# Column sums of the norm inside the last slab, high and low halves of the next weights moved, and sixteen unread products on TensorE

## The reference

```python
for l in range(2):
    sh, sc, gt = adaln(cond, w_ada[l], b_ada[l])      # one set for context, one for latent tokens
    h = y * (1.0 + sc) + sh
    o = even_mixer(h, ...) if l == 0 else odd_mixer(h, ...)
    y = layernorm(ALPHA * y + gt * o, ln_g[l], ln_b[l])
```

## Time and profile before

| | us |
|---|---|
| median of 3 runs | 2573.54 |
| lowest, highest | 2573.10, 2576.51 |
| the profiled execution | 2572.51 |
| its span, first to last instruction | 2570.9 |
| TensorE busy | 2521.2 (98%) |
| VectorE, ScalarE, GpSimd busy | 1943.4, 929.9, 924.0 |
| mean granted TensorE clock | 0.99 |

### The profile page before, as it was taken

The page is one execution under the profiler, slowest core; times in us unless marked ns, Lnnn a source line. Parts: engine busy times, 40 slices in busy tenths (PEclk is TensorE's granted clock), DMA queues, the critical chain, the costliest instruction groups (busy, mean ns, idle before and its releaser), DMA issues.

```text
span 2570.9 us, 40327 instructions
## 1 busy us (share of the span) xinstructions
PE 2521.2 (98%) x14518; PEld 2471.1 (96%) x14518; DVE 1943.4 (76%) x3355; ACT 929.9 (36%) x1184; POOL 924.0 (36%) x618
## 2 busy tenths in 40 slices
PE   6999999999999999999999999999999999999997
PEld 2699999999999999999999999999999999999997
DVE  2388888888888888889632389999999999474213
ACT  1233333333333333334322354433333333463223
POOL 0021111110111111111344566666666666572544
PEclk8999999999999999999999999999999999999998
DMA  9875656555665555564544434433333433563332
GB/s 391 328 229 184 203 186 197 190 186 197 200 201 197 194 186 190 191 205 152 165 140 136 139 110 138 138 129 132 132 130 130 137 129 129 180 209 131 124 124 89
DMA packets 131567, 442.02 MB, mean 172 GB/s; under 512 B 16720, under 2 KB 27216, under 8 KB 131456
## 3 DMA queue, kind: packets, MB, share of 16 engines
q1 hardware_dynamic: 114912, 409.23, 46.1%
q0 software_dynamic: 7328, 18.71, 3.8%
q10 hardware_dynamic: 9216, 12.59, 1.5%
HBM read 423.03 MB, written 15.18 MB: 170 GB/s over the span
## 4 chain that ended last, share of the span: by engine, by line
PE 90%; DVE 4%; DMA 3%; issue 1%; POOL 1%; ACT 1%; SPq 0%; ACTq 0%; DVEq 0%; POOLq 0%
PE bank L504 29%; PE bank L506 29%; PE bank L505 29%; DMA map<-in_w_ada_dram 3%; PE bank L603 1%; PE bank L520 1%; DVE w_lo L400 1%; PE bank L592 1%; DMA raw<-in_w_ada_dram 0%; DVE x L1290 0%; DVE o_lo L1149 0%; ACT w_hi L721 0%; POOL w_lo L400 0%; DVE part L1022 0%; POOL o L1510 0%
## 5 line engine op out<-in xcount | busy, mean ns | idle before, releaser
L504 PE MATMUL bank<-h_hi,w_hi 128*128 128x384 f32 x3543 | 1191.9, 336 | 2.1 <-DVE h_lo L959 1.9
L506 PE MATMUL bank<-h_hi,w_lo 128*128 128x384 f32 x3543 | 1184.5, 334 | 0.0
L505 PE MATMUL bank<-h_lo,w_hi 128*128 128x384 f32 x3543 | 1184.3, 334 | 0.0
L721 ACT ACTIVATE w_hi<-raw 128x1024 fp32r<-128x1024 f32 x572 | 595.0, 1058 | 860.1 <-PE bank L506 624.0
L400 POOL TENSOR_TENSOR w_lo<-raw,w_hi 128x1024 fp32r<-128x1024 f32 x247 | 604.3, 2462 | 544.9 <-ACT w_hi L721 542.6
L504 PEld LDWEIGHTS bank<-h_hi,w_hi 128*128 128x128 f32 x3543 | 665.6, 188 | 21.0 <-issue 15.8
L505 PEld LDWEIGHTS bank<-h_lo,w_hi 128*128 128x128 f32 x3543 | 665.7, 188 | 0.6
L506 PEld LDWEIGHTS bank<-h_hi,w_lo 128*128 128x128 f32 x3543 | 665.4, 188 | 0.0
L400 DVE TENSOR_TENSOR w_lo<-raw,w_hi 128x1024 fp32r<-128x1024 f32 x325 | 396.3, 1236 | 270.9 <-ACT w_hi L721 251.9
L1366 DVE SCALAR_TENSOR_TENSOR bank<-up,cw,bank 128x399 f32<-128x399 f32 x896 | 487.0, 626 | 0.0
L504 PE MATMUL bank<-o_hi,w_hi 128*128 128x384 f32 x1024 | 343.2, 335 | 1.4 <-DVE w_lo L400 0.9
(11 more groups left out here) (180 smaller groups left out, 1504.1 us busy)
## 6 DMA issues: line engine op xcount, KB each, us to landing
raw<-in_w_in_even_dram SPq DMA_DIRECT2D x256, 512.0 KB, 4.2
raw<-in_w_in_odd_dram SPq DMA_DIRECT2D x192, 512.0 KB, 3.3
raw<-in_w_ada_dram SPq DMA_DIRECT2D x120, 512.0 KB, 4.1
map<-in_w_ada_dram SPq DMA_DIRECT2D x64, 512.0 KB, 12.9
raw<-in_w_out_even_dram SPq DMA_DIRECT2D x64, 512.0 KB, 3.6
raw<-in_w_out_odd_dram SPq DMA_DIRECT2D x64, 512.0 KB, 3.2
gates<-sg ACTq DMA_DIRECT2D x32, 192.0 KB, 1.9
lg<-gates ACTq DMA_DIRECT2D x32, 192.0 KB, 3.7
```

The lines of the kernel that those rows point to most:

```text
L504: pe.matmul(out, w_hi[slot][:, t, :], hi[:, kk, :], start=(kk == 0), stop=False)
L505: pe.matmul(out, w_hi[slot][:, t, :], lo[:, kk, :], start=False, stop=False)
L506: mm = pe.matmul(out, w_lo[slot][:, t, :], hi[:, kk, :], start=False, stop=last)
L721: act.activation(w_hi[mine][:], raw[slot][:], ACT.Copy).then_inc(hi_ready, 1)
```

## The change

- In both layers, the columns of `total` and `energy` are now made inside the last slab of the output projection, between its seventh and eighth block (`summed_columns`); `token_moments` keeps those of block 15 and its square.
- In the norm of layer 0 TensorE makes 4 + 4 + 8 matmuls of 128x128 by 384 into strip 0 (`stay_awake`), whose results nothing reads: 4 behind the square columns, 4 behind the spread of the mean, 8 behind that of rstd. Each group waits for a free bank and for odd slab 0, which are there already.
- ScalarE makes `w_hi` of odd slab 2 ahead of the square of block 15, and behind the root only that of slab 3. For blocks 0 to 2 (`TOP_DIRECT`) it makes `h_hi` straight from the scaled `x` with two activations (context and latent part), and then the latent part of `made`, which VectorE still needs for `h_lo`.
- VectorE's wait for the stores of keys and values and its two memsets of `up` stand behind the norm instead of ahead of it.
- GpSimd makes `w_lo` of odd slab 1 ahead of adding block 14 instead of behind it, and that of slab 2 ahead of the DMA of `conf_w` instead of behind it.

```diff
@@ -614,6 +614,11 @@
             def out_projection(ph, layer):
                 for i in range(ph.bodies):
                     for k in range(ph.nw):
+                        if i == ph.bodies - 1 and k == ph.nw - 1:
+                            slab(ph, i, k, o_hi, o_lo, None, 0, SLAB_K - 1)
+                            summed_columns(2 * layer)
+                            slab(ph, i, k, o_hi, o_lo, None, SLAB_K - 1, SLAB_K)
+                            continue
                         slab(ph, i, k, o_hi, o_lo, (osplit_ready, KE * layer) if i == 0 and k % 4 == 0 else None)
                         if i == 1 and k == 2:
                             pe.wait_ge(z_added, 4 * layer + 1)
@@ -633,21 +638,39 @@
                     ins = pe.transpose(bank[b][:, n * P:(n + 1) * P], column[:, n:n + 1].to_broadcast([P, P]), eye)
                 return ins
 
-            def token_moments(call, src, count):
+            def summed_columns(call):
 
                 pe.wait_ge(total_ready, CLEARED[call] + CALLS[call])
                 token_columns(B_S1, total, True, False)
                 pe.wait_ge(energy_ready, CLEARED[call] + CALLS[call])
                 token_columns(B_S0, energy, True, False)
+
+            def token_moments(call, src, count):
+
                 pe.wait_ge(z_ready, count + KD)
                 token_columns(B_S1, src[:, KD - 1, :], False, True).then_inc(sums_ready, 1)
                 pe.wait_ge(squared, BEFORE[call] + KD)
                 pe.wait_ge(square_used, BEFORE[call] + KD - 1)
                 token_columns(B_S0, square[(KD - 1) % 2], False, True).then_inc(square_used, 1)
+                if call == 0:
+                    stay_awake(4)
                 pe.wait_ge(mean_col_ready, call // 2 + 1)
                 spread(B_S1, mean_col).then_inc(mean_spread, 1)
+                if call == 0:
+                    stay_awake(4)
                 pe.wait_ge(rstd_ready, call + 1)
                 spread(B_S0, rstd_col).then_inc(rstd_spread, 1)
+                if call == 0:
+                    stay_awake(8)
+
+            def stay_awake(count):
+
+                odd, ready = ODD.low(0, 0)
+                pe.wait_ge(bank_free[ODD.bank(0, 0)[0]], ODD.bank(0, 0)[1])
+                pe.wait_ge(lo_ready[odd], ready)
+                slot, out = ODD.w(0, 0) % RING, STRIP[ODD.bank(0, 0)[0]][:, 0:T]
+                for n in range(count):
+                    pe.matmul(out, w_hi[slot][:, 0, :], o_hi[:, KE - 1, :], start=True, stop=True)
 
             def gathered(call):
 
@@ -810,6 +833,8 @@
                             for k in TOP_STEPS.get(pair, ()):
                                 advance(k)
                         for t in ADDED.get((i, pair), ()):
+                            if t == KD - 1 and not layer:
+                                high_half(ODD, 0, 2)
                             square_of(2 * layer, t, x, z_ready, KD * layer)
                             if t == KD - 2:
                                 act.activation(rstd[:, T - 1:T], ones[:, 0:1], ACT.Sqrt)
@@ -834,13 +859,20 @@
 
             out_projection(OUT0, 0)
             root(0, rstd_col, var_col)
-            split_high(ODD, 0, 1)
+            high_half(ODD, 0, 3)
             for t in range(KD):
+                if t < TOP_DIRECT:
+                    act.wait_ge(scaled, t + 1)
+                    for c, (a, b) in enumerate(((0, TC), (TC, T))):
+                        ins = act.activation(h_hi[:, t, a:b], x[:, t, a:b], ACT.Identity,
+                                             bias=mod_next[:, 1, t, c:c + 1], scale=mod_next[:, 0, t, c:c + 1])
+                    ins.then_inc(top_ready, 1)
                 act.wait_ge(context_ready, t + 1)
                 act.activation(made[t % 3][:, TC:T], x[:, t, TC:T], ACT.Identity,
                                bias=mod_next[:, 1, t, 1:2], scale=mod_next[:, 0, t, 1:2]).then_inc(full_ready, 1)
-                act.wait_ge(full_ready, KD + t + 1)
-                act.activation(h_hi[:, t, :], made[t % 3], ACT.Copy).then_inc(top_ready, 1)
+                if t >= TOP_DIRECT:
+                    act.wait_ge(full_ready, KD + t + 1)
+                    act.activation(h_hi[:, t, :], made[t % 3], ACT.Copy).then_inc(top_ready, 1)
                 if t in (10, 11):
                     high_half(ODD, 0, t - 6)
 
@@ -1338,11 +1370,11 @@
 
             out_projection(OUT0, 0)
 
+            token_moments(0)
+            normalise_input()
             dve.wait_ge(kv_stored, 32 * HEADS)
             for e in range(2):
                 step(dve.memset(up[e][:], 0.0))
-            token_moments(0)
-            normalise_input()
             step(dve.memset(pivot[:], 0.0))
             for e in range(2):
                 step(dve.memset(acc[e], 0.0))
@@ -1518,10 +1550,10 @@
                         if first and layer:
                             odd_step(PAIRS_ODD + pair)
                         for t in ADDED.get((i, pair), ()):
+                            if ends and not last and t == POOLED - 1:
+                                low_half(pool, ph, i, 2 * pair + 3)
                             if t < POOLED:
                                 add_with_square(2 * layer, t, x, z_ready, KD * layer)
-                        if ends and not last:
-                            low_half(pool, ph, i, 2 * pair + 3)
 
                 if not layer:
                     pool.wait_ge(head_done, HEADS + 1)
@@ -1532,11 +1564,10 @@
 
             out_projection(OUT0, 0)
 
-            pool.dma_start(cw[:], conf_w).then_inc(conf_w_landed, 16)
-
             odd, ready = ODD.low(0, 0)
             pool.wait_ge(lo_ready[odd], ready)
             low_half(pool, ODD, 0, 2)
+            pool.dma_start(cw[:], conf_w).then_inc(conf_w_landed, 16)
             pool.wait_ge(mean_known, 1)
             for t in range(2, KD):
                 pool.tensor_tensor(x[:, t, :], x[:, t, :], pivot[:], ALU.subtract).then_inc(pool_centered, 1)
@@ -1571,6 +1602,7 @@
 TOP_STEPS = {0: range(15, 18), 1: range(18, 22), 2: range(22, 26), 3: range(26, 29), 4: range(29, KE)}
 LOW_STEPS = {0: range(8, 13), 1: range(13, 18), 2: range(18, 22), 3: range(22, 26), 4: range(26, 29), 5: range(29, KE)}
 EVEN_STEPS = 6 + PARTS * 3
+TOP_DIRECT = 3
 
 _pairs = [(j, a, q) for j in range(GROUPS) for a in range(2) for q in range(0, PARTS, 2)]
 UNITS = [(k, t) for q, t0 in ((0, 0), (0, 4), (1, 0)) for k in range(AHEAD * q, AHEAD * q + AHEAD) for t in range(t0, t0 + 4)]
```

## The result

| | before | after |
|---|---|---|
| median of 16 runs each, on the same chip in turns | 2574.18 | 2579.95 |
| lowest, highest | 2571.20, 2578.88 | 2576.58, 2582.10 |
| the profiled execution | 2572.51 | 2582.10 |
| its span | 2570.9 | 2580.5 |

The ratio is 1.0023, with a 95% interval of 1.0016 to 1.0029: the change makes the kernel 5.8 us slower. That lies just above the line of 0.2% (5.1 us), and the interval reaches to both sides of it. I had forecast 2578.1, which is 4.6 above the median that I then had.

What follows compares the result with a forecast made beforehand. TensorE was taken to bound the kernel, busy in 98% of the span, with VectorE's chain to block 12 deciding the passage between layers. 3.0 + 1.6 + 1.0 = 5.6 us on 2572.51 gave 2578.1 us, range 2574.5 to 2581.

Steps and rivals of the forecast that it cites:

- second rival: Layer 0's norm: the unread products keep TensorE's clock full, giving 2574.2 to 2575.8 us; chance 0.3 less likely half, 0.15.
- first rival: Layer 0's norm: the unread products run at the low clock all through, giving 2579 to 2581 us; chance 0.3.
- the forecast's case: Layer 0's norm: the clock falls 2.0 us after the last dense product, at 1471.5, so the first scaling comes 3.5 us later.
- block 12 is the gate: Passage between layers: TensorE waits 1.71 us for VectorE's low half of block 12, so VectorE's chain to it sets the time.
- Part 1: Layer 0's last slab: column sums inside it add 1.24 us to the slab and start the x columns 1.0 us later.
- Part 2: Layer 1's last slab: the same column sums move the end by +1.0 us (0 to 1.2; 1.0 more at low clock).
- Part 3: Layer 0's norm: unread products ahead of TensorE's waits delay the first scaling s0, +3.5 us taken, by when the clock falls.
- full-clock case: Layer 0's norm: with TensorE's clock full throughout, the first scaling comes at 1474.1, +1.2 us.
- the products hold the clock: Layer 0's norm: sixteen dense products in a former pause keep the clock full, 2574.2 to 2575.8 us; chance 0.15.
- Part 4: Layer 0's norm: slab halves made sooner end block 2's wait for GpSimd, -0.5 us; direct high halves 0, at most +0.2.
- Part 5: Waits for blocks 9 to 12: TensorE idles, its clock falls, costing 1.6 us behind block 12 (bounds 0 and 2.4).
- The sum: Whole kernel: 3.0 + 1.6 + 1.0 = 5.6 us on the profiled 2572.51, giving 2578.1 us.

Runs made afterwards that it cites:

- e5: After, with six more unread products ahead of block 11's wait and ten ahead of block 12's; median 2577.67 us, 1.0013 of before.
- e8: After, with TensorE doing slab 4 with blocks 8 to 10 ahead of block 11, and slab 4's low half made sooner; 2576.20 us, 1.0005 of before.
- e1_sums: Before, with only the total and energy columns moved inside the last slab, in both layers; median 2578.68 us, 1.0014 of before.
- r1: After, unchanged, run once more for a second trace; first scaling 12.88 us behind block 14's eviction, no median given.
- e2_awake: Before, with only the sixteen unread products added in layer 0's norm; median 2577.89 us, 1.0009 of before.
- e7: After, with only the last eight unread products, the four and four ahead of the spreads left out; median 2577.19 us, 1.0008 of before.
- r3: Before with only the column sums inside the last slab, second trace; 1109.60 us from layer 0's block 14 to the span's end, no median given.
- e3: Before, with only the moves on ScalarE, GpSimd and VectorE, nothing changed on TensorE; median 2574.29 us, 0.9998 of before.
- e4: After without the sixteen unread products; median 2576.75 us, 1.0006 of before.

## Why the prediction was right

The forecast was 2578.1 and +4.6 us; 2579.95 and +5.8 were measured, within the range of 2574.5 to 2581. (The second rival's start, 2574.2, lies a little below that range, not in it as I wrote.) By its number the result is not in the forecast's own range, which ended at 2579.2, but in that of the first rival, 2579 to 2581. In mechanism the first trace of after is the forecast's case: the clock fell at +8.1, behind the sums. The second is nearly the rival's: it fell at +7.0, and s0 is 4.1 us later. I had given "slower by over 0.2%" 0.36 and "within" 0.62, so the less likely side came, though the interval does not decide between the two. Point by point:

- **Where the time is decided** (TensorE is dense from 1500 on, block 12 is the gate, the ramp's slow clock before it costs nothing): right. Between the gate and the mark the distance is 39.63 to 39.66 us in all six traces without a fall there; what comes later at block 12 comes later at the mark. e5 and e8 show the other side of it, since filling the gate moves the mark at once.
- **Part 1, the sums in layer 0**: right in kind, a little small. Forecast 1.24 us for the slab and +1.0 for the x columns; measured 1.52 and +1.29. 1.34 of the 1.52 is there in layer 1 and in e1_sums too: the pairs take 1.26, as in a row of their own, and the first dense product behind them 0.09 more than usual, which I had not counted. 0.18 is the wait for GpSimd's energy sum, ready at 1470.77 and asked for a little sooner, where I had counted 0.1.
- **Part 2, layer 1**: forecast +1.0; +1.21 and +1.11 with the sums alone, +1.23 and +1.72 in the two traces of after. The clock fell on the second spread in e1_sums and the first trace of after (0.90 instead of 0.54 us), and on both in after's second. I had named that as an extra of up to 1.0.
- **Part 3, the products**: s0 forecast +3.5, measured +2.95 in the first trace and +4.1 in the second. Both are counted against the first trace of before; before itself moves by 0.8 (8.82, 8.05) and after by 1.6 (11.24 to 12.88 with the sixteen products in e5 and r1). What decides is the moment of the clock's fall, as said. The full-clock case, +1.2 by my sum, was seen in e8: +1.4 against the same trace. And its rival "the products hold the clock" came true there, in one of the five traces that had all sixteen; it is not shown that the products did it.
- **Part 4, the halves**: forecast -0.5, measured -0.6 and -0.95 from s0 to block 12 against the two traces of before. But it can't be added to part 3 as I did: e2_awake, without the halves, has the same 21.01 us from s0 to block 12 as after, because a later s0 already ends the wait for GpSimd. With the direct high halves TensorE's first product comes at s0 + 1.63; they were not run alone, and I see neither a cost nor a gain of theirs in the rows.
- **Part 5, the clock at the gate**: the fall came in all four traces (after twice, e2, e7) that had no more than 2 us of low clock in the ramp and nothing to fill the wait for block 12. It came in none of the six (before twice, e1, r3, e3, e4) whose ramp ran at the low clock for 3.7 to 5.6 us, and in neither e5 nor e8, where the wait was filled. The waits for blocks 10 to 12 add up to 2.7 to 2.9 us in the four and to 1.7 to 2.6 in the six, which is a narrow divide; that the wait is what matters is shown by e5. Its cost was mis-sized: 1.6 forecast, 2.75 and 1.5 measured. For a low stretch of 3.4 us the working holds (1.5 in r1_after, 1.6 in e7); but I took this shortest stretch as the likely one and 2.4 as the bound, and it was 6.8 us in the first trace and in e2 (2.75 and 2.5 us lost). The pause was also drawn too long: TensorE did not wait at block 9, and its own rows show 3.1 us of waits for h_lo (1.9 in before), not 4 and more.
- **The sum**, forecast 5.6 on the profiled execution: 5.09 to the mark, 1.23 at the end of layer 1, 0.7 between (0.5 of it late waits), 7.0 in this pair of traces; 5.8 in the medians. The profiled times themselves lie 9.6 apart, of which 2.5 arise ahead of block 14's eviction. That the total came near has some luck in it: in the first trace s0 was 0.55 sooner than forecast, and the fall 1.15 dearer.

## What to carry to other kernels

Unread products that are to hold TensorE's clock belong where no other engine waits for what stands behind them, and in front of work that sets the end. Here those ahead of the norm's spreads cost 0.85 us where the clock held (3.71 from the x columns to s0, against 2.86) and 1.7 where it fell at about the same moment in both programs (5.30 against 3.63), and sixteen at the gate won 2.8. Work moved "inside" a stage of an engine that has no idle time there lengthens that stage by all of it; behind the last product it was hidden beside VectorE's eviction for all but 0.25 us. And a faster clock or an earlier start ahead of a gate only makes the waits at the gate longer, and the clock can fall in them.

Two parts that act on the same wait can't be added: the moved halves gained 0.6 to 0.95 us by themselves and nothing beside the products.

## What the runs showed of the chip that I had not expected

- Twelve column sums (128x1 products with a full weight load each) between dense products take as long as in a row of their own: 1.26 us from the first to what follows, in both. The first dense product behind them then takes 0.26 instead of 0.17 us. In before's layer 0 and in after's layer 1 (the x columns follow in the one, dense products in the other):

```profile
1468.06 0.72 PE L627 MATMUL bank<-ones,total 128*128 128x1 f32 x6
...
1469.32 0.81 PE L627 MATMUL bank<-ones,x 128*128 128x1 f32 x6
```

```profile
2559.11 0.72 PE L632 MATMUL bank<-ones,total 128*128 128x1 f32 x6
...
2560.37 0.42 PE L504 MATMUL bank<-o_hi,w_hi 128*128 128x384 f32 x1
...
2560.63 0.34 PE L505 MATMUL bank<-o_lo,w_hi 128*128 128x384 f32 x1
```

  The Trainium skill (TensorE: Matmul & The Clock Gate, "Step-by-step: what each phase is for") has loads pulled ahead of running products; no row here shows that this saves anything for a series of twelve loads.
- The cost of one fall of the clock varies by a factor of two between executions of the same program: 6.8 and 3.4 us low at the same place in two traces of after, with 2.75 and 1.5 us lost.
- The sixteen unread products went with a clock that held in one trace of the five that had them (e8), and in the other four it fell between 6.3 and 8.8 us behind block 14's eviction, at the sums or just behind them.
